# A decoder trunk on one core: order of the first turns, and how expert outputs are stored and summed

## The reference

```
grp = argmax(t @ w_grp + b_grp)                 # one of 4 groups
top_v, top_i = top_k(expert logits of that group, 2)
gate = one_hot(grp) * softmax(top_v) * p_grp    # 512 x 16, two entries a token
for e in range(16):
    hdn = silu(t @ w_gate[e]) * (t @ w_up[e])
    y = y + gate[:, e:e + 1] * (hdn @ w_down[e])
h = h + y
```

## Time and profile before

| | us |
|---|---|
| median of three runs | 1459.06 |
| the profiled execution | 1462.68 |
| its span, first to last instruction | 1460.9 |
| TensorE busy | 1331.9 (91%) |
| VectorE busy | 1037.9 (71%) |
| ScalarE busy | 861.3 (59%) |
| POOL busy | 386.0 (26%) |

### The profile page before, as it was taken

How to read it: one execution, slowest core, us unless ns; L and a number is a source line. 1 busy time by engine, 2 the same in 40 slices (tenths; PEclk the granted TensorE clock), 3 DMA queues, 4 the chain that set the end, 5 groups by cost and what they waited for, 6 DMA issues and landing times. The chain is left out here.

```text
span 1460.9 us, 28467 instructions
## 1 busy us (share of the span) xinstructions
PE 1331.9 (91%) x10957; PEld 1052.4 (72%) x10957; DVE 1037.9 (71%) x1399; ACT 861.3 (59%) x1316; POOL 386.0 (26%) x433
## 2 busy tenths in 40 slices
PE   5899997888899899999996999999998899999994
PEld 2477776776754788888873887878786788888872
DVE  5556854557653799998996527666445899999986
ACT  6835644454521578888883434435543588888882
POOL 2022345456710122233314100011110133223313
PEclk9999999999999899999998999999979999999998
DMA  6322300311574599999993432112131799999985
GB/s 192 116 87 87 116 15 3 107 32 40 149 295 171 204 378 384 386 384 382 381 357 128 144 102 87 58 58 81 65 116 62 246 388 388 389 383 384 379 318 175
DMA packets 160822, 300.11 MB, mean 205 GB/s; under 512 B 17117, under 2 KB 32605, under 8 KB 160720
## 3 DMA queue, kind: packets, MB, share of 16 engines
q1 hardware_dynamic: 149264, 274.01, 52.2%
q0 software_dynamic: 11232, 24.61, 4.7%
q10 hardware_dynamic: 224, 0.07, 0.0%
HBM read 280.35 MB, written 34.60 MB: 216 GB/s over the span
## 5 line engine op out<-in xcount | busy, mean ns | idle before, releaser
L1703 DVE TENSOR_TENSOR moe_wlo<-kept_raw,moe_whi 128x2048 fp32r<-128x2048 f32 x162 | 370.2, 2288 | 40.9 <-ACT moe_whi L1699 36.4
L1699 ACT ACTIVATE moe_whi<-kept_raw 128x2048 fp32r<-128x2048 f32 x192 | 365.4, 1919 | 38.5 <-DMA kept_raw<-in_moe_w_down_dram 17.5
L1710 PE MATMUL all_bank<-moe_whi,moe_xhi 128*128 128x512 f32 x512 | 203.7, 398 | 3.5 <-DVE moe_xlo L1759 3.5
L1712 PE MATMUL all_bank<-moe_whi,moe_xlo 128*128 128x512 f32 x512 | 199.5, 390 | 0.0
L1711 PE MATMUL all_bank<-moe_wlo,moe_xhi 128*128 128x512 f32 x512 | 199.4, 389 | 0.0
L1710 PEld LDWEIGHTS all_bank<-moe_whi,moe_xhi 128*128 128x128 f32 x512 | 96.1, 188 | 25.6 <-issue 3.0
L1712 PEld LDWEIGHTS all_bank<-moe_whi,moe_xlo 128*128 128x128 f32 x512 | 96.1, 188 | 20.6
L1711 PEld LDWEIGHTS all_bank<-moe_wlo,moe_xhi 128*128 128x128 f32 x512 | 96.2, 188 | 18.8
L1710 PE MATMUL all_bank<-moe_whi,moe_hhi 128*128 128x512 f32 x256 | 100.9, 394 | 3.3 <-issue 2.6
L1712 PE MATMUL all_bank<-moe_whi,moe_hlo 128*128 128x512 f32 x256 | 100.4, 392 | 0.0
L1711 PE MATMUL all_bank<-moe_wlo,moe_hhi 128*128 128x512 f32 x256 | 100.4, 392 | 0.0
(11 more groups left out here) (464 smaller groups left out, 2935.4 us busy)
## 6 DMA issues: line engine op xcount, KB each, us to landing
kept_raw<-in_moe_w_gate_dram SPq DMA_DIRECT2D x64, 1024.0 KB, 11.0
kept_raw<-in_moe_w_up_dram SPq DMA_DIRECT2D x64, 1024.0 KB, 12.3
kept_raw<-in_moe_w_down_dram SPq DMA_DIRECT2D x64, 1024.0 KB, 11.3
attn_xhat<-in_w_kv_dram SPq DMA_DIRECT2D x10, 1024.0 KB, 5.1
out_dram<-kept_raw SPq DMA_DIRECT2D x16, 512.0 KB, 5.9
attn_xhat<-in_attn_w_q_dram SPq DMA_DIRECT2D x6, 1024.0 KB, 4.9
all_h<-in_rwkv_w_k_dram SPq DMA_DIRECT2D x4, 1024.0 KB, 9.2
all_h<-in_rwkv_w_v_dram SPq DMA_DIRECT2D x4, 1024.0 KB, 5.0
```

What stands on the lines that cost most here:

```text
L1699: nc.scalar.activation(whi[slot % SPLITS][:, :], raw[slot % 6][:, :], ACT.Copy).then_inc(m["hi_ok"], 1)
L1703: nc.vector.tensor_tensor(wlo[slot % SPLITS][:, :], raw[slot % 6][:, :], whi[slot % SPLITS][:, :].bitcast(fp32), ALU.subtract).then_inc(m[ ...
L1710: nc.tensor.matmul(bank[b][:, :], hi[:, k0 + k, :], wh[:, k, :], start=begin and k == 0, stop=False)
L1712: ins = nc.tensor.matmul(bank[b][:, :], lo[:, k0 + k, :], wh[:, k, :], start=False, stop=end and k == 3)
```

## The change

The start: the block of its own for the first constants goes, and POOL sets them in the project block (`first_constants`). TensorE turns the first three tiles of x first, then the parameter rows (into the bank square that the last turn will use), then the last tile. VectorE copies the parameters after it has normalised all four tiles.

The expert stage: the weight of each place in each list is worked out by eight small products (`weight_list`) from `share`, and kept in `slot_wgt`. ScalarE scales by it while it copies the output to `yo`. POOL stores by an indirect transfer that adds to its destination, `sum_dram` of the layer, at the token's own row. So `out_dram`, `pos`, `near` and the rows of the outputs go, and SP loads the sums back with four plain transfers. As many rows are zeroed beforehand as were before (16 tiles of 128 rows). The last expert's output is split into a high and a low part by halves (`act_last`, `dve_last`), and the selection makes two products of each; all first halves come ahead of all second halves.

```diff
@@ rwkv_project, TensorE
-            pe.wait_ge(par_in, 16 * 9)
-            nc.tensor.transpose(bank[7][:, 0:P], parrow[:, :], g["ident"][:, :]).then_inc(par_tr, 1)
-            pe.wait_ge(par_ok, 1)
+            pe.wait_ge(g["ready"], 4)
             for j in range(J):
+                if j == J - 1:
+                    pe.wait_ge(par_in, 16 * 9)
+                    nc.tensor.transpose(bank[7][:, P * j:P * j + P], parrow[:, :], g["ident"][:, :]).then_inc(par_tr, 1)
                 pe.wait_ge(xhat_ok, j + 1)
                 for kt in range(KT):
+                    if j == J - 1 and kt == KT - 1:
+                        pe.wait_ge(par_ok, 1)
@@ moe
+        def weight_list(b, rows):
+            for k in range(2):
+                for j in range(J):
+                    ins = nc.tensor.matmul(bank[6][:, NE * b:NE * b + NE], rows[:, k, j, :].bitcast(fp32), share[:, k, j, :], start=k == 0 and j == 0, stop=k == 1 and j == J - 1)
+            return ins
-            nc.scalar.activation(yo[:, 512 * half:512 * half + 512], bank[5 + half][:, :], ACT.Copy).then_inc(m["y_ok"], 1)
+                act.wait_ge(m["wgt_ok"], c + 1)
+            nc.scalar.activation(yo[:, 512 * half:512 * half + 512], bank[5 + half][:, :], ACT.Copy, scale=wgtcol[:, :]).then_inc(m["y_ok"], 1)
+        def act_last(act, half, n):
+            act.wait_ge(main["piece_used"], n + main["lead"] + 1)
+            nc.scalar.activation(yhi[half], bank[5 + half][:, :], ACT.Copy, scale=slot_wgt[:, LASTE:NE]).then_inc(last_hi, 1)
+        def dve_last(dve, half):
+            dve.wait_ge(last_hi, half + 1)
+            nc.vector.scalar_tensor_tensor(out=ylo[half], in0=bank[5 + half][:, :], scalar=slot_wgt[:, LASTE:NE], in1=yhi[half].bitcast(fp32),
+                                           op0=ALU.mult, op1=ALU.subtract).then_inc(last_lo, 1)
             pool.wait_ge(m["y_ok"], c * 2 + 3)
             pool.sem_inc(turn, 1)
-            pool.indirect_dma_start(out_dram, bass.IndirectOffsetOnAxis(ap=outcol[:, :], axis=0), yo[:, :], None,
-                                    bounds_check=NE * T - 1, oob_is_err=False).then_inc(m["y_st"], 16)
+            if m is main:
+                weight_column(pool, m, col + 1)
+            pool.indirect_dma_start(dst, bass.IndirectOffsetOnAxis(ap=outcol[:, :], axis=0), yo[:, :], None,
+                                    bounds_check=T - 1, oob_is_err=False, compute_op=ALU.add).then_inc(m["y_st"], 16)
@@ moe, SP
+            def sums(src):
+                for j in range(J):
+                    sp.dma_start(xn[:, j, :], src[P * j:P * j + P, :]).then_inc(comb_in[j], 16)
+            sp.wait_ge(main["y_st"], 16 * LASTE)
+            sums(sum_dram)
@@ moe, VectorE
+            shares()
+            for k, Mk in enumerate([M1, M2]):
+                V.tensor_tensor(share[:, k, :, :], flat(Mk), wgt[:, k, :].rearrange("p (j x) -> p j x", x=1).to_broadcast([P, J, NE]), ALU.mult).then_inc(share_ok, 1)
             dve.wait_ge(first_sent, 1)
...
             dve_tokens(dve, main, 0, 0)
+            dve.wait_ge(share_mm, 1)
+            V.tensor_copy(slot_wgt[:, 0:NE], bank[6][:, 0:NE]).then_inc(slot_ok, 1)
...
-            for j in range(J):
-                combine(j, near, 1, comb_ok)
-                if j:
-                    add_last(j - 1)
-            add_last(J - 1)
+            for x in range(2):
+                for j in (2 * x, 2 * x + 1):
+                    combine(j, 1, comb_ok)
+                dve_last(dve, x)
+            dve.wait_ge(comb_ok, J)
+            for half in range(2):
+                for j in range(J):
+                    add_last(j, half)
@@ moe, TensorE
-            for j in range(J):
-                for half in range(2):
-                    nc.tensor.matmul(last_bank(j, half)[:, :], picksT[:, j, :], yo[:, 512 * half:512 * half + 512], start=True, stop=True).then_inc(last_mm, 1)
+            for half in range(2):
+                pe.wait_ge(last_lo, half + 1)
+                for j in range(J):
+                    nc.tensor.matmul(last_bank(j, half)[:, :], picksT[:, j, :], yhi[half], start=True, stop=False)
+                    nc.tensor.matmul(last_bank(j, half)[:, :], picksT[:, j, :], ylo[half], start=False, stop=True).then_inc(last_mm, 1)
```

More of the change, by code:

```diff
@@ L236, in sem, with first_constants @@
         return self.sems[-1]
+def first_constants(nc, pool, g):
+    ch = Chain(pool, g["ready"])
+    ch.inc(nc.gpsimd.memset(g["eps"][:, 0:1], NORM_EPS))
+    ch.inc(nc.gpsimd.memset(g["eps"][:, 1:2], GN_EPS))
+    ch.link(nc.gpsimd.memset(g["ident"][:, :], 0.0))
+    ch.link(nc.gpsimd.affine_select(out=g["ident"][:, :], in_=g["ident"][:, :], compare_op=ALU.not_equal, fill=1.0, base=0,
+                                    pattern=[[-1, P]], channel_multiplier=1))
 def constants(nc, pool, g, sem):
@@ L615, in _ @@
         def _(act):
+            act.wait_ge(g["ready"], 2)
             nc.scalar.activation(ss[:, 0:1], g["eps"][:, 0:1], ACT.Sqrt).then_inc(root_in, 1)
@@ L980, in _ @@
             sp.wait_ge(blank_ok, 1)
-            for e in range(16):
-                blank_rows(e)
+            for name in ("sum_dram0", "sum_dram1", "spare_dram0", "spare_dram1"):
+                for j in range(J):
+                    blank_rows(name, j)
             wait(sp, "s_ok", NC - 1, 4)
@@ L1854, in _ @@
                 each_further(sp, further_round)
+                sp.wait_ge(more["y_st"], 16 * NE * (J - 1))
+                sp.wait_ge(comb_ok, J)
+                sums(spare_dram)
             if result is not None:
@@ L1962, in _ @@
             for half in range(2):
-                act_output(act, main, NE - 1, half, piece(NE, 0, half)[0])
+                act_last(act, half, piece(NE, 0, half)[0])
             with overflow(act):
@@ L2135, in round_, with combine, add_last @@
                 part_lo(*then(3), 0)
-            def combine(j, weights, taken, done):
-                dve.wait_ge(comb_in[j], 32 * taken)
-                for k in range(2):
-                    src = (xn if k == 0 else xnT2)[:, j, :]
-                    V.scalar_tensor_tensor(out=h[:, j, :], in0=src, scalar=weights[:, k, j:j + 1], in1=h[:, j, :], op0=ALU.mult, op1=ALU.add).then_inc(done, 1)
-                    dve.wait_ge(done, 2 * j + k + 1)
-            def add_last(j):
-                for half in range(2):
-                    dve.wait_ge(last_mm, 2 * j + half + 1)
-                    hh = h[:, j, 512 * half:512 * half + 512]
-                    V.scalar_tensor_tensor(out=hh, in0=last_bank(j, half)[:, :], scalar=last_wgt[:, j:j + 1], in1=hh, op0=ALU.mult, op1=ALU.add).then_inc(last_ok, 1)
+            def combine(j, taken, done):
+                dve.wait_ge(comb_in[j], 16 * taken)
+                V.tensor_tensor(h[:, j, :], xn[:, j, :], h[:, j, :], ALU.add).then_inc(done, 1)
+            def add_last(j, half):
+                dve.wait_ge(last_mm, J * half + j + 1)
+                hh = h[:, j, 512 * half:512 * half + 512]
+                V.tensor_tensor(hh, last_bank(j, half)[:, :], hh, ALU.add).then_inc(last_ok, 1)
             rounds(dve, round_)
@@ L2898, in build @@
             io[f"xn_dram{i}"] = nc.dram_tensor(f"xn_dram{i}", [T, D], fp32).ap()
-        io["out_dram"] = nc.dram_tensor("out_dram", [16 * T, D], fp32).ap()
-        io["y_dram"] = nc.dram_tensor("y_dram", [T, D], fp32).ap()
+        for i in range(2):
+            for x in ("sum", "spare"):
+                io[f"{x}_dram{i}"] = nc.dram_tensor(f"{x}_dram{i}", [T, D], fp32).ap()
         io["v_dram"] = nc.dram_tensor("v_dram", [T, D], fp32).ap()
-        with nc.Block() as block:
-            @block.gpsimd
-            def _(pool):
-                ch = Chain(pool, g["ready"])
-                ch.inc(nc.gpsimd.memset(g["eps"][:, 0:1], NORM_EPS))
-                ch.inc(nc.gpsimd.memset(g["eps"][:, 1:2], GN_EPS))
-                ch.link(nc.gpsimd.memset(g["ident"][:, :], 0.0))
-                nc.gpsimd.affine_select(out=g["ident"][:, :], in_=g["ident"][:, :], compare_op=ALU.not_equal, fill=1.0, base=0,
-                                        pattern=[[-1, P]], channel_multiplier=1)
         with Scope(nc, "rwkv") as s:
```

122 lines of the change are left out of this document (47 added, 75 removed).

## The result

The changed kernel took 1478.64 us (median of 4 runs, 1475.35 to 1485.19), the kernel before beside it 1461.15 us; the ratio is 1.013, 95% interval 1.009 to 1.017. Slower by some 17 us, where 1457.5 was forecast; the range ended at 1477. The profiled execution took 1475.35 us, its span is 1473.4 us, 12.5 us more than before.

A forecast was written before the change was run, and what follows sets the result against it. It held DMA time at the end of each expert stage to be exhausted. Terms -5.0 + (-1.5 + 9.2 - 5.5) + (-1.0 + 9.2 - 6.9) = -1.5 us gave 1457.5 us for the median; likeliest 1451 to 1465, full range 1439 to 1477.

The forecast's parts named there:

- Which resource: End of each expert stage: no DMA time to spare, so added DMA time is paid one to one.
- Head: Kernel start: turning x ahead of the parameter rows saves 5.0 us (bounds 3.5 to 5.6).
- Starts of the stages: Start of each expert stage: fewer small VectorE instructions, -1.5 us in the first, -1.0 us in the second.
- Tails: Ends of both stages: plain loads of sums and fewer additions, -5.5 us in the first, -6.9 us in the second.
- The rival of late sums: Tails don't shrink: sums land late behind the last store, four us later in each tail, 1465.5 us; chance 0.08.
- The accumulating stores: Expert stages: the added read costs extra DMA time, +9.2 us a stage, bounds 0 to +18.
- one store costs 0.66 us of the core's DMA time: Expert stages: price of one plain store, from POOL's queue share of 16 engines' time.
- as much again: Expert stages: an accumulating store's added read costs another 0.66 us, +9.2 us a stage.
- f: Extra DMA time of an accumulating store in units of a plain one; time 1439.2 + 18.4 f, forecast 0.7 to 1.4.
- The second rival: Expert stages: accumulating is slower than twice a plain store; 1476 us at f = 2; chance 0.25.
- four rows per engine: Expert-stage weight-load ring, second rival: each engine's four rows are read, added and written before the next load's packet.
- the forecast of 10% for POOL's queue: First expert stage, 515 to 769 us: POOL's queue share rises from 7.1% to about 10% at f = 1.

The follow-up runs named there:

- c_head: The kernel before with only the start changed (first constants in the project block, x turned ahead of the parameter rows): 1454.82 us, ratio 0.997.
- a_plain: The changed kernel with plain stores in place of accumulating ones, so a token's second expert overwrites its first: 1439.29 us, ratio 0.985.
- q_64slots: The changed kernel with its accumulating store cut to the first 64 list entries, rows past 64 not stored: 1434.81 us, ratio 0.984.
- m_linear: a_plain plus a second store of each expert output, sent directly by ScalarE as 64 whole rows without an index list: 1457.68 us.
- d_twice: a_plain plus a second plain indirect store of each expert output to a spare tensor: 1478.66 us.
- n_perm: The changed kernel, accumulating stores kept, with the iota row permuted so an expert's tokens spread over its 128 slots: 1473.38 us, ratio 1.010.
- r_split: The changed kernel with each accumulating store in two, by lists of slots 0 to 63 and 64 to 127, one after the other: 1503.01 us, ratio 1.029.
- u_fetch: The changed kernel with the token fetch split into two lists of 64 slots from the fourth expert on: 1492.26 us, ratio 1.022.
- h_two: The changed kernel without accumulation: first and second choices stored plainly in two tensor halves, both added in the tail: 1447.55 us, ratio 0.992.
- g_norows: The changed kernel with plain stores and a second plain store of each output whose bound lets through token 0 alone: 1438.37 us.
- l_none: a_plain with a bound that lets only token 0 through, so hardly any row is stored: 1437.2 us.

## Why the prediction was wrong

*Which resource.* Right, and it carried the study: no DMA time to spare, so anything added is paid one to one.

*Head.* Right: -5.3 us in the trace, 5.1 us alone (c_head), 5.0 forecast.

*Starts of the stages.* -1.5 us was forecast for the first. In the two profiled executions ScalarE's first work of the stage moved from 475.82 to 465.63 us (-10.2) and TensorE's turn of the third expert's tokens from 513.40 to 500.51 (-12.9). The granted clock was 0.74 in 480 to 500 us before and 0.83 in 460 to 480 us after, so some of the 2.7 us is clock, and the term can't be read off. Taken as the rest of a_plain's 20.6 us (5.1 for the head, 14.4 for the tails below) both starts gave 1.1 us, where 2.5 was forecast.

*Tails.* Forecast -5.5 and -6.9 us. From the last output copy to the last square or scale the first fell from 15.6 to 9.5 us (-6.2), the second from 21.5 to 13.3 (-8.2). The rival of late sums did not happen: VectorE waited 0.99 us for the first and 0.85 us for the last one. In the second tail the eight additions of banks took 4.86 us where 5.4 was granted, and the squares followed each other at 1.37 us, not at 1.57.

*The accumulating stores.* **This step failed: "one store costs 0.66 us of the core's DMA time", and with it "as much again" for the added read, +9.2 us a stage.** The loss is 39.3 us, 19.6 a stage, f = 2.1 in the prediction's unit; by 1439.2 + 18.4 f, f = 2.1 gives 1478 us, which is the time. The second rival's number came true ("At f = 2 the time is 1476 us"), not its reason; that is luck. The factor between an added and a plain row was about right: records of single packets have 159 ns for a plain row of 4 KB and 327 ns for an added one, 2.06. That is near the 1.93 that the Trainium skill gives for the bandwidth of a copying against a reducing collective ("Collectives: The Full Stack", "The bandwidth ceiling"). What was mis-sized by two is the unit. I had divided the queue's packet time by sixteen engines, and wrote of "four rows per engine"; with 64 of 128 slots filled it is eight rows on eight engines. The added read is then 8 x 168 ns on these, in place of 4. With that, one figure for each run, over 28 stores in the DMA-bound part:

| | rows on the busiest engine, ns each | us a store | x 28 | measured |
|---|---|---|---|---|
| addition (after over a_plain) | 8 x (327 - 159) | 1.34 | 37.6 | 39.3 |
| a second, a third plain store | 8 x 159 | 1.27 | 35.6 | 39.4, 36.3 |
| the second by half rows | 8 x 80 | 0.64 | 17.9 | 19.6 |
| 64 rows of a direct transfer | 4 x 159 | 0.64 | 17.8 | 18.4 |
| addition by a list of 64 | 4 x 327 - 8 x 159 | 0.04 | 1 | -4.5 |

(80 ns is half of 159, an estimate. The last row ends at TensorE's floor, so its two figures are not of one kind.) That the busiest engine sets the price is shown by q_64slots against the change and m_linear against d_twice. That eight engines take the first 64 slots is shown by the chains of packets and by the shorter stores of n_perm. What no run shows is a kernel that stores every row, adds, and has four rows on an engine: r_split ended at GpSimd. u_fetch, which did the same for the fetch, went the other way, only in part for reasons that its trace shows.

*What the views could have told.* That the forecast of 10% for POOL's queue came true with double the loss says how little that share can carry: it is a mean over engines. The sign of trouble in the trace before was there: stores of 0.26 MB took 7.1% of sixteen engines, but how many engines held them I never asked.

*The range.* It missed by 1.6 us, because I put f = 2 as the last bound when the text itself named "and more".

## What to carry to other kernels

Where DMA engines bind, price a small transfer by its busiest engine, not by its queue's mean share: an index list of 128 with some 60 filled entries cost 1.3 to 1.4 us a store where 64 rows, sent directly, cost 0.66. Keep an index list no longer than the rows in it. Or place the filled entries where all engines get some: by the rule under n_perm, rows in slots 0 to 31 and 64 to 95 would put four on each of sixteen engines, an estimate that no run has tried. And ask whether an addition can wait for an engine that has time: two plain halves summed in the tail gave 1447.6 us, where adding on the way cost 1478.6 and the kernel before took 1460.6. Before splitting a transfer in two, count the round of the queue that waits for it.

## What the runs showed of the hardware

- A row of 4 KB took 159 ns as a packet when stored and 327 ns when added to its destination; alone on the engines, the last store of a stage landed as little as 3.2 us after its issue plain (h_two) and 6.1 us added (the change).
- By a list of 128 entries, runs of four slots go to the engines, slots 0 to 63 to eight of them: 75 rows stood in eight chains of 8 and three of 4, 4 and 3 (a_plain, h_two). Beside weight loads no more than 7 to 9 rows were under way at once for up to 67 filled entries; by a list of 64 there were 13 to 18.
- An empty entry is still a packet, of 4 bytes in a plain store and 8 in an added one, some 7 to 9 ns long. It cost nothing that 28 stores show (g_norows, 1438.4 us; l_none, 1437.2 us).
- Two stores of GpSimd of which the second must follow the first took 7.7 and 7.8 us of its round (r_split).
- Rows fetched by two lists of 64 took 207 ns as packets, 160 by one list of 128 (u_fetch against the change, 520 to 700 us).
